# Half-piece seams, rotated banks, interleaved units and spread warm-up products in a five-layer token kernel

## The reference, cut

```python
def first_block(x, ...):
    mix = token_mixer(x, w_in, b_forget, rel_bias, w_out)   # fox heads, band heads, then @ w_out
    x = layer_norm(2 ** 0.25 * x + mix, ln1_g, ln1_b)
    ffn = conv_ffn(x, w_up, conv_w, conv_b, w_down)         # width 2816, conv of 3, gelu gate
    return layer_norm(2 ** 0.25 * x + ffn, ln2_g, ln2_b)

def second_block(x, ...):
    y = retention_mla_layer(x, ...)   # 4 retention heads, 8 latent heads, @ w_out_even (3072 rows)
    x = layer_norm_2(4 ** 0.25 * x + y, ...)
    y = moba_layer(x, ...)            # 16 heads; with 256 tokens one own block, causal
    return layer_norm_2(4 ** 0.25 * x + y, ...)
```

## Time and profile before

| | us |
|---|---|
| median of 3 runs | 776.27 |
| lowest, highest | 775.65, 778.67 |
| the profiled execution | 776.75 |
| its span, first to last instruction | 774.9 |
| TensorE busy | 754.0 |
| VectorE busy | 528.6 |
| ScalarE busy | 381.5 |
| mean granted clock of TensorE | 0.994 |

### The profile page before, as it was taken

One profiled execution on the slowest core, in us unless ns is written; L12 is line 12 of the kernel. 1 busy time (PEld: TensorE's weight loads), 2 busy tenths in 40 slices (PEclk: granted clock), 3 DMA queues, 4 the chain that ended last, 5 costly groups with the idle time before them and its releaser, 6 DMA issues.

```text
span 774.9 us, 12675 instructions
## 1 busy us (share of the span) xinstructions
PE 754.0 (97%) x4838; PEld 662.1 (85%) x4838; DVE 528.6 (68%) x940; ACT 381.5 (49%) x627; POOL 35.3 (5%) x50
## 2 busy tenths in 40 slices
PE   8999998999999999999999999999899999999995
PEld 8987876899999988889999777987678879997974
DVE  4655667687778854857686566965374587878756
ACT  5655662486566664256554444433433424556450
POOL 0000001021111200100000000000000010000001
PEclk9999999999999999999999999999999999999998
DMA  8952435446555596256536344553566616435502
GB/s 304 322 183 82 136 118 210 136 150 210 174 184 188 182 299 197 84 196 209 167 97 200 128 135 136 158 185 128 181 212 214 213 68 217 164 121 182 163 27 81
DMA packets 37580, 130.62 MB, mean 169 GB/s; under 512 B 4304, under 2 KB 4688, under 8 KB 37392
## 3 DMA queue, kind: packets, MB, share of 16 engines
q1 hardware_dynamic: 36144, 125.09, 48.8%
q0 software_dynamic: 1232, 4.46, 2.0%
q10 hardware_dynamic: 144, 0.26, 0.1%
HBM read 128.74 MB, written 1.05 MB: 167 GB/s over the span
## 4 chain that ended last, share of the span: by engine, by line
PE 94%; DVE 3%; issue 1%; ACT 1%; DMA 1%; DVEq 0%; SPq 0%
PE acc L812 28%; PE acc L814 27%; PE acc L813 27%; PE acc L929 2%; PE acc L948 2%; PE acc L968 2%; PE acc L987 1%; PE acc L927 1%; PE acc L1000 1%; DVE w_lo L1272 1%; PE acc L935 1%; DMA res<-in_x 1%; PE acc L1011 1%; PE acc L961 0%; PE acc L1026 0%
## 5 line engine op out<-in xcount | busy, mean ns | idle before, releaser
L1272 DVE TENSOR_TENSOR w_lo<-raw,w_hi 128x1024 fp32r<-128x1024 f32 (+1 forms) x223 | 260.7, 1197 | 73.1 <-ACT w_hi L1106 72.1
L1106 ACT ACTIVATE w_hi<-raw 128x1024 fp32r<-128x1024 f32 (+1 forms) x223 | 224.4, 1035 | 90.1 <-PE acc L814 79.4
L812 PE MATMUL acc<-X_hi,w_hi 128*128 128x256 f32 x848 | 242.9, 286 | 0.0
L813 PE MATMUL acc<-X_lo,w_hi 128*128 128x256 f32 x848 | 239.9, 283 | 0.0
L814 PE MATMUL acc<-X_hi,w_lo 128*128 128x256 f32 x848 | 239.8, 283 | 0.0
L812 PEld LDWEIGHTS acc<-X_hi,w_hi 128*128 128x128 f32 x848 | 162.5, 192 | 5.2 <-issue 4.8
L813 PEld LDWEIGHTS acc<-X_lo,w_hi 128*128 128x128 f32 x848 | 162.6, 192 | 0.5 <-issue 0.2
L814 PEld LDWEIGHTS acc<-X_hi,w_lo 128*128 128x128 f32 x848 | 162.6, 192 | 0.0
L812 PE MATMUL acc<-w_hi,S_hi 128*128 128x512 f32 x256 | 102.5, 400 | 2.5 <-DVE gate L1339 2.5
L813 PE MATMUL acc<-w_lo,S_hi 128*128 128x512 f32 x256 | 100.2, 391 | 0.0
L814 PE MATMUL acc<-w_hi,S_lo 128*128 128x512 f32 x256 | 100.0, 390 | 0.0
(11 more groups left out here) (165 smaller groups left out, 793.3 us busy)
## 6 DMA issues: line engine op xcount, KB each, us to landing
raw<-in_w SPq DMA_DIRECT2D x225, 512.0 KB, 4.2
raw<-in_w SPq DMA_DIRECT2D x11, 256.0 KB, 3.0
gate<-in_ln_gain POOLq DMA_DIRECT2D x4, 512.0 KB, 5.0
gate<-in_ln_bias POOLq DMA_DIRECT2D x4, 512.0 KB, 5.5
res<-in_x SPq DMA_DIRECT2D x4, 256.0 KB, 4.4
gate<-in_bias SPq DMA_DIRECT2D x1, 1024.0 KB, 8.3
out<-res SPq DMA_DIRECT2D x4, 256.0 KB, 2.0
decay<-in_decay SPq DMA_DIRECT2D x1, 512.0 KB, 6.8
```

What stands on the lines that cost most here:

```text
L812: nc.tensor.matmul(out, a_hi, b_hi, start=start, stop=False)
L813: nc.tensor.matmul(out, a_hi, b_lo, start=False, stop=False)
L1106: nc.scalar.activation(home(u, "hi")[:, 0:n], raw[:, u % RAW, 0:n], ACT.Copy).then_inc(hi_done, 1)
L1272: nc.vector.tensor_tensor(home(u, "lo")[:, 0:n], raw[:, u % RAW, 0:n], home(u, "hi")[:, 0:n].bitcast(F32), ALU.subtract).then_inc(lo_done, 1)
```

## The change

It has six edits. (1) Layer one's chunks: qB0 comes before vB, and kB1 and qB1 become four chunks of one unit, kB10, qB10, kB11, qB11; band jobs 8 to 11 name kB0 and qB0, jobs 12 and 13 kB10 and qB10, jobs 14 and 15 kB11 and qB11. (2) `between`: its first step is emitted before the last early half piece, the second where both were. (3) For the late pieces, low-half splits are emitted to one piece less than high-half splits. (4) out2 begins at bank 2 (first token half in banks 2 and 3, second in 0 and 1; `bank_of` wraps) and runs with early=2. (5) The second ry turn of a head uses job bank 2 instead of 0. (6) The warm-up products: four, then one behind each of the first three transposes, instead of three and four.

```diff
+def bank_of(first, x):
+
+    return first + x if first >= 4 else (first + x) % 4
...
-        add(f"{name}{half}", "F", 2, "X", k8, "act", ("copy_feat", name[0], s, half),
+        add(f"{name}{half}", "F", 2, "X", k8, "act", ("copy_feat", name[0], s, 2 * half, 2),
             ("w_in", None, cols(c0 + 256 * half, 256)))
...
     feat("qA", QA, 0, 1)
+    feat("qB", QB, 1, 0)
     add("vB", "A", 4, "X", k8, "act", ("copy_tok", 1), ("w_in", None, cols(VB, 512)))
-    feat("qB", QB, 1, 0)
-    feat("kB", KB, 1, 1)
-    feat("qB", QB, 1, 1)
+    for unit in (2, 3):
+        for name, c0 in (("k", KB), ("q", QB)):
+            add(f"{name}B1{unit - 2}", "F", 1, "X", k8, "act", ("copy_feat", name, 1, unit, 1),
+                ("w_in", None, cols(c0 + P * unit, P)))
...
-    add("out2", "B", 24, "S", list(range(24)), "dve", ("norm", 2), ("w_out_even", list(range(16, 24)) + list(range(16)), None))
+    add("out2", "B", 24, "S", list(range(24)), "dve", ("norm", 2), ("w_out_even", list(range(16, 24)) + list(range(16)), None), at=2)
...
             at = ch.get("at", (at + w - 1) // w * w % 4)
-            ch["bank"], ch["before"] = at, {b: held[b] for b in range(at, at + w) if held[b] is not None}
-            for b in range(at, at + w):
+            banks = [bank_of(at, x) for x in range(w)]
+            ch["bank"], ch["before"] = at, {b: held[b] for b in banks if held[b] is not None}
+            for b in banks:
                 held[b] = c
             at = (at + w) % 4
...
-    JOBS.append(dict(kind="band", s=1, h=h, qk=[f"kB{h // 4}", f"qB{h // 4}"], v="vB", g=None, tile=4 + h // 2))
+    u = "0" if h < 4 else f"1{h // 2 - 2}"
+    JOBS.append(dict(kind="band", s=1, h=h, qk=[f"kB{u}", f"qB{u}"], v="vB", g=None, tile=4 + h // 2))
...
-            if early and half == (0, 1):
-                for st in between:
-                    emit(st)
+            if between and half in ((early - 1, 0), (0, 1)):
+                emit(between[half[1]])
...
-                split_to(min(u + AHEAD + 2 if part == 0 else NU, ch["u0"] + n - late + RING + (name != "out3") * 4))
+                to = ch["u0"] + n - late + RING + (name != "out3") * 4
+                split_to(min(u + AHEAD + 2 if part == 0 else NU, to), ("hi",))
+                split_to(min(u + AHEAD + 1 if part == 0 else NU, to), ("lo",))
...
-            t = new_t(("ry", r, i), ("S", 8 + 4 * r + i), True, 3 if i == 0 else 0, r, 2)
+            t = new_t(("ry", r, i), ("S", 8 + 4 * r + i), True, 3 if i == 0 else 2, r, 2)
...
-    for st in (tok0[0], tok1[0], tok0[1], tok1[1]):
+    for i, st in enumerate((tok0[0], tok1[0], tok0[1], tok1[1])):
         emit(st)
-    emit(("warm", 1))
+        if i < 3:
+            emit(("warm", i + 1))
...
-    for name in ("qA1", "vB", "qB0", "kB1", "qB1"):
+    for name in ("qA1", "qB0", "vB", "kB10", "qB10", "kB11", "qB11"):
...
-    run("out2", 1, lambda i: {f"L2y{i}"}, tail=turn_x(3, 0), inside={(4, 0): [("load", "ln", 2)]})
+    run("out2", 1, lambda i: {f"L2y{i}"}, early=2, tail=turn_x(3, 0), inside={(4, 0): [("load", "ln", 2)]})
...
-                if b < 2 and kind == "norm":
+                if bank_of(0, b - old["bank"]) < 2 and kind == "norm":
...
-                    chunk_waits(pe, c, (2 * part, 2 * part + 1))
+                    chunk_waits(pe, c, [bank_of(b0, 2 * part + x) for x in (0, 1)])
...
-                for _ in range((3, 4)[n]):
+                for _ in range((4, 1, 1, 1)[n]):
```

More of the change, by code:

```diff
@@ L879, in mm @@
                         w = slice(nn * n, (nn + 1) * n)
-                        last = three(acc[:, b0 + tt * 2 + nn, 0:n], hi[:, k, tt * P:(tt + 1) * P],
+                        last = three(acc[:, bank_of(b0, tt * 2 + nn), 0:n], hi[:, k, tt * P:(tt + 1) * P],
                                      lo[:, k, tt * P:(tt + 1) * P], wh[:, w], wl[:, w], i == 0, i == len(tiles) - 1)
@@ L1142, in evac @@
                 if kind == "copy_feat":
-                    _, which, s, half = e
-                    dst = (qT if which == "q" else kT)[s][:, 2 * half:2 * half + 2, :]
-                    nc.scalar.activation(dst, acc[:, b0, :].rearrange("p (a s) -> p a s", a=2), ACT.Copy)\
+                    _, which, s, first, units = e
+                    dst = (qT if which == "q" else kT)[s][:, first:first + units, :]
+                    nc.scalar.activation(dst, acc[:, b0, 0:units * S].rearrange("p (a s) -> p a s", a=units), ACT.Copy)\
                         .then_inc(evac_act, 1)
@@ L1464, in norm_sum @@
                     res[:, tt, q * 512:(q + 1) * 512], res[:, tt, q * 512:(q + 1) * 512],
-                    ALPHA1 if ch["evac"][1] < 2 else ALPHA2, acc[:, ch["bank"] + 2 * tt + q, :], ALU.mult, ALU.add)
+                    ALPHA1 if ch["evac"][1] < 2 else ALPHA2, acc[:, bank_of(ch["bank"], 2 * tt + q), :], ALU.mult, ALU.add)
                 if (tt, q) == (1, 1):
```

## The result

The changed kernel took a median of 768.16 us in five executions (767.65 to 768.52), the kernel before beside it 777.08 (775.65 to 778.96): a ratio of 0.9879, 95% interval 0.9862 to 0.9897. The forecast was 768.2, in a range from 766.0 to 771.9. The profiled execution took 768.47 us, 8.28 less than the one before (776.75), and its span is 766.7; the sum had given 768.6 for it.

A forecast was written before the change was run, and what follows sets the result against it. TensorE bounds it, busy 754.0 of 774.9 us; only its waits and low-clock time can go. Terms of -4.4, -1.45, -0.8, -2.5, +1.33 and -0.35 sum to -8.17: 768.6 from 776.75, forecast 768.2, range 766.0 to 771.9 us.

The forecast's parts named there:

- The seams: At up01, rv0 and mv0: splitting the eight transposes around a half piece gains 0.48 us each, -1.45 in all.
- The slip of 0.49 us: At each seam, the moved low split (1.16 us) in VectorE's chain, less 0.67 of waiting, delays X by about 0.49 us.
- out1: Layer one's last chunks: waits of 2.7 us go, plus 1.7 us of low clock behind them, -4.4 in sum.
- Rival 2: out1 stays bound by VectorE: half of 4.4 stays, the seams give nothing; 771.85 us, chance 0.09.
- The clock: Behind out1's waits TensorE ran at 0.66 for 5 us; without the wait no fall, 1.70 us gained.
- rival 1: The clock dip near 120 us is absent from most executions before, so 1.7 us less gain: 769.9 us, chance 0.15.
- Layer two: Retention turn in bank 6 gives -0.8; out2's rotated banks and early=2 remove the wait for rg3's gate, -2.5.
- out3's new wait: At out3's first product: rotated banks put it over mgt11, whose gate it must await, +1.33 us.
- The sign that would have made the forecast wrong: Another L812 wait behind a chunk whose bank moved; a wait over 1 us at out1 was the alternative sign.
- Rival 3: Order changes less than derived: transposes 14, 15 still late, out3's wait as large as out2's old one; 773.7 us, chance 0.08.
- rival 4: out3's new wait drops TensorE to 1.2 GHz and it stays there: 782 us, chance 0.04.
- The start: Warm-up products spread between transposes: from +0.1 to -0.7 us depending on when the clock rises, taken as -0.35.

The follow-up runs named there:

- Experiment 1: The changed kernel with low halves of late pieces emitted to the same piece as the high halves, as before: 766.47 us, ratio 0.9861 to the kernel before.
- experiment 3: The kernel before with only layer one's new chunk order and single units: 774.55 us, ratio 0.9958 to the kernel before.
- experiment 2: The changed kernel with layer one's chunks in the old order, all else of the change kept: 769.18 us, ratio 0.9894 to the kernel before.
- Experiment 4: The kernel before with only out2's rotated banks and its early=2: 775.67 us, ratio 0.9984 to the kernel before.
- experiment 7: The changed kernel with b_forget loaded early on ScalarE's queue instead of SyncE's: 767.61 us, ratio 0.9871 to the kernel before.

## Why the prediction was right, point by point

**The seams** were right term by term: -1.45 us forecast, -0.51, -0.48 and -0.46 measured (16.42 to 16.44 before, 15.93 to 15.96 after). The slip of 0.49 us from the low split that moved into the chain of the first token half measured 0.48, and TensorE's own path ended the seam, as derived. Experiment 1 confirms the slip by taking it out.

**out1** was right in its mechanism and 0.2 us high: -4.4 forecast, -4.20 measured. The wait that it starts from, on TensorE in the kernel before:

```profile
119.76 0.52 PE L948 MATMUL acc<-cst,pr 128*128 128x128 f32 x3 [1.97 <-DVE S_lo L1431]
```

If the fall cost there what it cost in experiment 3 (1.58), the waits gave 2.62 of their 2.7. Rival 2, that VectorE would still bound it, fell: VectorE is busier there than before (5.00 of 5 us), but with nothing that TensorE waits for. What I had not seen is that the two edits cover each other. The order alone removes the whole wait (experiment 3), the later low halves with the old order remove 1.5 of 2.7 us and the clock fall (experiment 2), so with the order in place they are a pure cost of 1.5 us at the seams.

**The clock** was right in its sum, though for a reason that was only half of it. I took the fall as tied to the waits at out1, with rows 13 as evidence that the wait at out2 is harmless. Experiment 3 shows that it isn't: the same 2.5 us wait cost 1.6 us more where it ended 3.7 us earlier (555.21 against 558.91). The Trainium skill's rule ("TensorE: Matmul & The Clock Gate", What's actually happening) that a transition depends on a phase which the program does not set fits this pair of profiles, though no run here measures the phase. What I drew from it was wrong, though: rival 1 said that most executions of before would have no fall. Of the 17 beside experiment 3, seven show a mean granted clock of 0.992, nine 0.994 or 0.995 and one 0.996; the profiled one, with its single fall, has 0.994. The seven had a median of 778.95 us, the seven at 0.994 776.84. One fall lowers the mean by 0.002 (half speed for 3.4 of 775 us) and costs 1.7 us, so it is likely that the slower ones had two; none of them was profiled. The count is rough: every profile also ends at the low level, for its last 3.6 to 6.9 us, when TensorE has no work left (0.50 from 770 us to the end in the kernel before), and that alone moves the mean by up to 0.002. The changed kernel's five show 0.996 or 0.997. Rival 1 fell the other way round: before, most executions seem to have one fall or two, and few none. A part of the measured gain, 8.9 us between medians against 8.3 between the two profiles, may be this.

**Layer two** was forecast at -0.8 - 2.5 = -3.3 and gave -4.13. This is the largest miss, and it is a term mis-sized, not a cause missed. The second head's retention scores show it, for which the list of waits has no line at all. TensorE's timeline of the kernel before:

```profile
471.16 0.39 PE L813 MATMUL acc<-w_lo,X_hi 128*128 128x512 f32 x1
471.39 0.40 PE L814 MATMUL acc<-w_hi,X_lo 128*128 128x512 f32 x1
471.90 1.10 PE L1011 MATMUL acc<-qT,kT 128*128 128x256 f32 x4
472.84 0.61 PE L1013 MATMUL acc<-qT,kT 128*128 128x128 f32 x4
```

And of the changed kernel:

```profile
466.06 0.39 PE L824 MATMUL acc<-w_lo,X_hi 128*128 128x512 f32 x1
466.29 0.39 PE L825 MATMUL acc<-w_hi,X_lo 128*128 128x512 f32 x1
466.52 1.02 PE L1022 MATMUL acc<-qT,kT 128*128 128x256 f32 x4
467.38 0.61 PE L1024 MATMUL acc<-qT,kT 128*128 128x128 f32 x4
```

From the last pass to the scores 0.51 us against 0.23, and from the first to the second group of scores 0.94 against 0.86: the stop cost 0.28 + 0.08 = 0.36 us. The view of idle time sees only 0.11 of it (471.39 + 0.40 to 471.90), since the pass before is still draining in the first 0.17, and the first instructions behind a stop come further apart by 0.08. So this stop cost a quarter of a microsecond more than the view shows, and the same working gives 1.02 us for the last head's scores (0.77 listed) and 2.74 for out2 (2.47 listed): 0.36 + 1.02 + 2.74 = 4.12 us, against 4.13 in the ledger. It is no rule for every stop: out3's wait (1.33 listed) cost 1.39 in the ledger, and the waits at out1 gave no more than they list. Rows 2 should have been read with the distances of starts around each wait. Experiment 4 repeats it: -2.80 with the bank edit alone, where 2.5 is listed.

**out3's new wait** was forecast at 1.33 us with the gate as releaser; the trace has 1.33, and the ledger +1.39. The sign that would have made the forecast wrong, another such wait behind a chunk whose bank moved, did not appear. Rival 3 (smaller effects of the order) and rival 4 (the clock falls there and stays) did not occur: a stop of 1.33 us left the clock at full speed.

**The start** was forecast at -0.35, and this pair of profiles shows +0.12. Part two of the first products did come sooner than I had worked out (12.0), at 10.58, and the clock rose sooner, as the rates show (16 transposes and six constant passes took 3.2 us from 5.14, the 16 transposes alone 3.5 before). The gain was then lost on VectorE to the load of b_forget, which landed at 17.38 in this profile and at 17.04 before: a step that I had not followed beyond 12 us. Where the load landed sooner, the first scores came sooner by the same amount (the six profiles under experiment 7). Medians put the edit at 0.2 to 1.0 us, so -0.35 may be a fair mean, but by a path that I had not worked out. The term was small enough not to matter, but it is the one that I can't call right.

In sum -4.20 - 1.45 - 4.13 + 1.39 + 0.12 - 0.01 = -8.28, where -8.17 was forecast. The agreement to 0.1 is luck: layer two gave 0.8 more, the start 0.5 and out1 0.2 less. The step from the sum to the forecast was luck too: it took 0.5 us off because the profiled execution of before lay that far above the median of three, and with five executions it lies 0.3 below their median (776.75 against 777.08).

## What to carry to other kernels

Weigh each part by the distance between landmarks of the written order in two profiles, not by the list of waits, which here left out a quarter of a microsecond of three stops and nearly nothing of others, and not by whole times, which the start and the clock blur. Of two edits made against one wait, try each alone: here the second was not needed and cost 1.5 us elsewhere. And when a counter that hands out banks is shifted at one place, follow it to the end of the program: the last user of it paid 1.4 us of the 2.8 that were won, and one argument gave them back.

## What the runs showed of the hardware

The length of a stop alone does not decide whether the clock falls behind it. One wait of 2.5 us for the same gate was followed by full speed in the kernel before and by 3.4 us at 1.2 GHz in experiment 3, where it ended 3.7 us earlier in the execution; waits of 0.5 and 0.7 us (experiment 2) and of 1.33 us (out3) were followed by full speed in every profile that has them. The kernel before, with waits of 2.0 and 2.5 us, also has the wider spread of times: 775.7 to 779.4, against 767.4 to 768.5 in the changed kernel. That the clock is the cause of this spread is likely by the mean clocks above, but not shown.

The third load of x (256 KB), issued at 2.1 us in every profile, landed between 6.4 and 7.8 us, and the 0.5 KB of b_forget took 6.0 us behind weight pieces on SyncE's queue (4.6 to 6.0 over the profiles) and 3.9 to 4.1 us as an early load on ScalarE's.
